# Hybrid decoder step on one Trainium2 core: order of work in the two inner layer norms, the state update on VectorE, and the wait for the last gated chunk

## The chip, the cores and the metric

One core of a Trainium2 chip runs the whole program. The time is device microseconds of that core for one launch. The core has TensorE (matmuls, called PE in the profile), VectorE (DVE), ScalarE (ACT), GpSimd (POOL) and SyncE (SP), which only issues transfers. Each engine is a queue that works in order; they are tied together by semaphores alone. Of the kernel before there are three timed runs and one profiled execution.

## The reference

One inference step of a hybrid decoder layer on 256 prompt tokens and 8 sample tokens, 264 columns in all, model width 2048, everything in float32:

```
h  = layer_norm(ALPHA * x  + mixer(x),            ln 0)   # gated DeltaNet heads + block-sparse attention
h  = layer_norm(ALPHA * h  + cross_attend(h),     ln 1)   # 4 heads, 256 memory tokens
y  = layer_norm(ALPHA * h  + swiglu(h),           ln 2)   # (silu(h W1a) * (h W1b)) W2, hidden 5632
layer_norm(x) = (x - mean(x)) * rsqrt(var(x) + 1e-5) * g + b
# recurrent state of every sample token b and head:
S  = S * exp(g_b) + k_b (outer) u_b
```

The mean and the variance are taken over the 2048 features of each token. The new states S of the eight samples (8 heads of 128 x 128 each) are an output too.

## The kernel before

**Layout.** Activations lie with features on the 128 partitions: `xf` is 16 chunks of 128 features by 264 tokens. Every float32 product is made from three faster ones: weights and activations are split into a rounded upper part (`wh`, `xh`) and the rest (`wl`, `xl`), and TensorE adds `wh*xh + wh*xl + wl*xh` (lines 504 to 506).

**Units.** A unit is one 128-column output tile: 16 chunks of weights, 1 MB, and 48 matmuls into one half of `psum_g`. For each unit SP loads `raw` (`load_unit`, line 477), ScalarE makes the upper part `wh` (`upper`, line 481), VectorE the low part `wl` (`lower`, line 486), and TensorE multiplies (`unit`, line 512). There are two slots of each. `upper` of unit U waits until unit U-2 has left TensorE; a load waits until the low part of two units before is made. `upper_next` and `lower_next` prepare the unit after the one named. The order of all that is written out by hand in each engine's program; nothing reorders it. The stages, with their units, are: `out` (16, mixer output), `wk` (4, memory keys), `xq` (4, queries), `wv` (4, memory values), `xo` (4, attention output), then `w1a` 32, `w2a` 16, `w1b` 32, `w2b` 16, `w1c` 24, `w2c` 16.

**Layer norm i** is spread over three engines. TensorE sums over the features by matmuls with a matrix of ones: sum in bank 0 of `M`, sum of squares in bank 1 (`gathered`, `last_sum`, `last_square`, lines 2118 to 2137). VectorE (line 1635) makes mean, mean square, variance and maximum with 0; ScalarE (line 1085) turns it into `rstd` by Ln and Exp. The 16 chunks are worked in five groups (`LN_PARTS`: 2, 2, 4, 4, 4 chunks): VectorE centres and scales a group, ScalarE applies g and b (line 1096) and rounds it to `xh` (line 1103), VectorE makes `xl` (line 1664). Layer norm 0 stands beside the four `wk` units, which need only the memory tokens; so the upper and low parts of the next units and the copies of finished keys (`memory_keys`, line 1118) are placed between the groups. The first `xq` unit waits group by group for the low parts. Layer norm 1 has no such unit beside it: the first `w1a` unit follows it. Between them ScalarE loads its table for Silu (line 1092).

**Before layer norm 1**, the four `xo` units each make four output chunks (banks 0 to 3 of `M`, or 4, 5 and both halves of `psum_g`). VectorE adds each to the residual `xf` and gathers sums in `xt[:, 8:12]` and squares in `xt[:, 12:16]`.

**Gate stages** (`w1a`, `w1b`, `w1c`): units come in pairs, gate and up. ScalarE makes Silu of the first, VectorE the product and its upper and low part, `gh` and `gl` (`gate_unit`, lines 1788 to 1800). **Residual stages** (`w2a`, `w2b`, `w2c`) multiply the 16 (or 12) gated chunks; their loops begin behind one wait for all low parts (line 2260).

**State update.** In `w1a`, 32 units in four turns of eight, the states of the eight samples are updated, one per four units: Pool loads state and rows into `state` and `ub`; VectorE scales the state (line 1811), ScalarE scales the rows by k, one instruction for each of 8 heads (line 1186), VectorE adds (line 1816), Pool stores. They hang on the semaphores `h_act` and `h_dve`.

Of the kernel before, what the change touches and what calls it, by code (L numbers as in the profile page):

```python
# [30 lines left out]
ACT = mybir.ActivationFunctionType  # L31
ALU = mybir.AluOpType
AXX = mybir.AxisListType.X
ds = bass.ds
# [7 lines left out]
H = 8  # L42
# [91 lines left out]
def build(nc, a, o):  # L134

    ctx = ExitStack()
    with ctx:
# [274 lines left out]
        h_act, h_dve = steps("h_act", ["k"]), steps("h_dve", ["g", "s"])  # L412
# [11 lines left out]
        NG = len(LN_PARTS)  # L424
        l_pe = steps("l_pe", ["sum", "var"])
# [6 lines left out]
        x_pe = steps("x_pe", ["sc", "ss", "pt", "st", "v0", "out", "v1", "so"])  # L432
        x_act = steps("x_act", ["exp", "sexp", "pt", "mv", "oh", "row0", "row1", "soh"])
        x_dve = steps("x_dve", ["qz", "mx", "smx", "rc", "src", "spn", "pn", "xpz", "mv", "ol", "row2", "row3", "sol"])
# [146 lines left out]
        def _(sp):  # L581
# [232 lines left out]
        def _(act):  # L814
# [270 lines left out]
            def layer_norm(i, between={}):  # L1085
# [5 lines left out]
                if i == 1:  # L1091
                    act.preload_act_table(ACT.Silu)
                for g, part in enumerate(LN_PARTS):
# [10 lines left out]
                    if g in between:  # L1104
                        between[g]()
# [12 lines left out]
            def memory_keys(u):  # L1118
# [47 lines left out]
            for u in range(4):  # L1166
                upper_next(act, turn, u)
                act.wait_ge(psum_free, 4 * turn + u + 3)
                if u >= 2:
                    act.wait_ge(sq_added, SUMS[1] + u - 1)  # L1170
                nc.scalar.activation(xt[:, 4 * (u % 2):4 * (u % 2) + 4], xf[:, 4 * u:4 * u + 4],
                                     ACT.Square).then_inc(sq_made, 1)
            layer_norm(1)
            turn, n = STAGES["w1a"]
            with act.Fori(0, n // 2) as i:
                for s in range(2):
                    for u in range(4):
                        upper_next(act, i * 2 + (turn + s), u)
                        if u % 2 == 0:
                            unit_done(act, i * 2 + (turn + s), u)  # L1180
                            act.wait_ge(psum_free, i * 8 + (4 * (turn + s) + u + 2))
# [7 lines left out]
            for s1_, s2_, first, nk in GROUPS:  # L1189
                if s1_ != "w1a":  # L1190
                    turn, n = STAGES[s1_]
                    with act.Fori(0, n) as i:
                        for u in range(4):
                            upper_next(act, i + turn, u)
                            if u % 2 == 0:
                                unit_done(act, i + turn, u)
                                act.wait_ge(psum_free, i * 4 + (4 * turn + u + 2))
                                nc.scalar.activation(sg[:], psum_g[:, 0, 0:T], ACT.Silu).then_inc(psum_free, 1)  # L1198
# [1145 lines left out]
```

## Time and profile before

| | |
|---|---|
| timed runs | 1705.89, 1713.7, 1715.07 us; median 1713.7 |
| profiled execution | 1706.84 us, of which the span from first to last instruction is 1705.2 |
| TensorE busy | 1583.8 us (93%), 14865 matmuls, mean granted clock 0.978 |
| VectorE, ScalarE busy | 886.2 us (52%), 648.8 us (38%) |
| low parts, line 489 | 223 instructions, mean 2287 ns |
| upper parts, line 484 | 223 instructions, mean 1874 ns |
| first matmul of a chunk, line 504 | idle 58.0 us before it, 24.2 of them for the low part of the weights |

How to read it: the busy time of TensorE counts overlapping records, so it is not the array's use; what counts is where it stands idle, and what ended that idle time. The last column of a timeline row, in brackets, is the idle time of the engine before the instruction and the instruction that ended it. The clock is given as a share of full speed.

### The profile page before, as it was taken

The page shows a single profiled execution, that of the slowest core. Times are in us where ns is not written, and L with a number is a line of the kernel's source. Part 1 is how long each engine was busy: PE and PEld are TensorE (multiplying, and loading weights), DVE is VectorE, ACT ScalarE, POOL GpSimd, SP SyncE. Part 2 cuts the span into 40 slices and gives each one's busy share as a digit, 9 for nine tenths or more (in the row PEclk, how much of TensorE's full clock was granted, in tenths as well). Part 3 has the DMA queues.
Part 4 walks back from the last instruction along what each step waited for, and adds up shares of the span by engine and source line. Part 5 has one row for each costly group of instructions (what it writes and reads, how often), then busy time and mean ns, then how long its engine had stood idle before and what let it go on. Part 6 is the DMA issues. An engine that isn't in the chain of part 4 may idle for free.

```text
span 1705.2 us, 36365 instructions
## 1 busy us (share of the span) xinstructions
PE 1583.8 (93%) x14865; PEld 1534.6 (90%) x14865; DVE 886.2 (52%) x992; ACT 648.8 (38%) x756; POOL 200.9 (12%) x298
## 2 busy tenths in 40 slices
PE   5989999999899879988978999999999999999996
PEld 5988999999889779987778999999999999999996
DVE  2435555656744246654476555444454444454466
ACT  3433334243422534443355344333333333333344
POOL 0001112121587501000100110000000000000000
PEclk9999999999999999988999999999999999999998
DMA  5589878685688967433644756545545544554443
GB/s 213 180 327 361 333 271 311 249 312 190 186 245 256 297 248 296 173 123 127 247 145 164 259 209 237 190 173 176 190 175 175 194 172 174 179 189 175 169 155 121
DMA packets 104415, 365.10 MB, mean 214 GB/s; under 512 B 14369, under 2 KB 48490, under 8 KB 77290
## 3 DMA queue, kind: packets, MB, share of 16 engines
q1 hardware_dynamic: 88978, 322.26, 53.2%
q0 software_dynamic: 12528, 37.24, 6.4%
q10 hardware_dynamic: 2800, 4.09, 0.8%
q8 instruction: 75, 1.23, 0.3%
q14 instruction: 34, 0.28, 0.0%
HBM read 353.27 MB, written 10.47 MB: 213 GB/s over the span
## 4 chain that ended last, share of the span: by engine, by line
PE 69%; issue 8%; DVE 7%; ACT 6%; SPq 3%; DMA 3%; POOL 2%; POOLq 1%; ACTq 1%; DVEq 0%
PE psum_g L504 20%; PE psum_g L505 19%; PE psum_g L506 19%; PE M L1910 4%; PE M L1895 3%; DVE wl L489 3%; ACT wh L484 3%; SPq L599 2%; PE psum_g L2193 1%; DMA raw<-w_out_t 1%; POOL pj L576 1%; ACT xf L1096 1%; ACT ub L1186 1%; DMA kring<-cache_k_t 1%; SPq L632 1%
## 5 line engine op out<-in xcount | busy, mean ns | idle before, releaser
L504 PE MATMUL psum_g<-xh,wh 128*128 128x264 f32 x2640 | 777.7, 295 | 58.0 <-DVE wl L489 24.2
L505 PE MATMUL psum_g<-xl,wh 128*128 128x264 f32 x2640 | 755.1, 286 | 0.0
L506 PE MATMUL psum_g<-xh,wl 128*128 128x264 f32 x2640 | 754.0, 286 | 0.0
L489 DVE TENSOR_TENSOR wl<-raw,wh 128x2048 fp32r<-128x2048 f32 (+1 forms) x223 | 510.1, 2287 | 445.7 <-ACT wh L484 445.4
L504 PEld LDWEIGHTS psum_g<-xh,wh 128*128 128x128 f32 x2640 | 503.9, 191 | 75.8 <-DVE wl L489 26.8
L484 ACT CAST wh<-raw 128x2048 fp32r<-128x2048 f32 (+1 forms) x223 | 417.8, 1874 | 318.0 <-PE psum_g L506 267.9
L505 PEld LDWEIGHTS psum_g<-xl,wh 128*128 128x128 f32 x2640 | 504.6, 191 | 3.4 <-issue 3.2
L506 PEld LDWEIGHTS psum_g<-xh,wl 128*128 128x128 f32 x2640 | 501.9, 190 | 0.0
L504 PE MATMUL psum_g<-gh,wh 128*128 128x264 f32 x704 | 202.0, 287 | 6.0 <-DVE gl L1798 6.0
L506 PE MATMUL psum_g<-gh,wl 128*128 128x264 f32 x704 | 200.9, 285 | 0.0
L505 PE MATMUL psum_g<-gl,wh 128*128 128x264 f32 x704 | 200.8, 285 | 0.0
L504 PEld LDWEIGHTS psum_g<-gh,wh 128*128 128x128 f32 x704 | 134.0, 190 | 6.8 <-issue 6.6
L505 PEld LDWEIGHTS psum_g<-gl,wh 128*128 128x128 f32 x704 | 134.1, 190 | 0.0
L506 PEld LDWEIGHTS psum_g<-gh,wl 128*128 128x128 f32 x704 | 133.4, 190 | 0.0
L1910 PE MATMUL M<-chain 128*128 128x128 f32 x704 | 90.2, 276 | 0.0
L1910 PEld LDWEIGHTS M<-chain 128*128 128x128 f32 x704 | 85.2, 193 | 0.0
L1895 PE MATMUL M<-kring,pj 128*32 128x128 f32 x1536 | 63.8, 277 | 9.9 <-DMA sraw<-cache_k_t 5.2
L1895 PEld LDWEIGHTS M<-kring,pj 128*32 128x32 f32 x1536 | 55.4, 111 | 15.6 <-issue 12.5
L744 POOL TENSOR_TENSOR chain<-chain,C 128x512 f32<-128x512 f32 x28 | 43.0, 1537 | 122.4 <-PE M L1910 101.1
L576 POOL DMA_DIRECT2D pj<-cache_v x102 | 54.7, 538 | 10.8 <-issue 6.1
L1836 DVE SCALAR_TENSOR_TENSOR xf<-xf,psum_g 128x264 f32 (+1 forms) x48 | 20.6, 429 | 64.8 <-PE psum_g L506 64.5
L1198 ACT ACTIVATE sg<-psum_g 128x264 f32<-128x264 f32 x28 | 11.0, 391 | 111.1 <-PE psum_g L506 111.1
(380 smaller groups left out, 1312.0 us busy)
## 6 DMA issues: line engine op xcount, KB each, us to landing
raw<-w_t SPq DMA_DIRECT2D x88, 1024.0 KB, 4.8
raw<-w_in_t SPq DMA_DIRECT2D x55, 1024.0 KB, 6.7
kring<-cache_k_t SPq DMA_DIRECT2D x96, 512.0 KB, 4.5
sraw<-cache_k_t SPq DMA_DIRECT2D x32, 512.0 KB, 6.0
raw<-w_out_t SPq DMA_DIRECT2D x16, 1024.0 KB, 4.8
raw<-w2a_t SPq DMA_DIRECT2D x16, 1024.0 KB, 4.8
raw<-w2b_t SPq DMA_DIRECT2D x16, 1024.0 KB, 4.7
raw<-w2c_t SPq DMA_DIRECT2D x16, 768.0 KB, 4.2
```

The costliest lines, as they stand in the source:

```text
L484: nc.scalar.copy(wh[:, u % 2, 0:nk], raw[:, u % 2, 0:nk]).then_inc(hi_done, 1)
L489: eng.tensor_tensor(wl[:, u % 2, 0:nk], raw[:, u % 2, 0:nk], wh[:, u % 2, 0:nk].bitcast(F32), ALU.subtract).then_inc(raw_used, 1)
L504: nc.tensor.matmul(out, hi_w, x_hi(k), start=(k == order[0]), stop=False)
L505: nc.tensor.matmul(out, hi_w, x_lo(k), start=False, stop=False)
L506: last = nc.tensor.matmul(out, lo_w, x_hi(k), start=False, stop=(k == order[-1]))
L576: eng.dma_start(v_pages[s][:, t], a["cache_v"][0, ds(pages[6 * n_ + t], 1), :, h].rearrange("a t d -> t (a d)"))\
L599: _, pages = nc.values_load_multi_w_load_instructions(page_turns[4 * i + u:4 * i + u + 1], engines={mybir.EngineType.SP}, min_val=0, max_v ...
L632: sp.dma_start(state_half(b, s), a["state_dn"][0, b, 4 * s:4 * s + 4].rearrange("h d e -> d h e"))\
L744: nc.gpsimd.tensor_tensor(cm, at0, over(mask), ALU.mult).then_inc(b_pool.sem, 1)
L1836: nc.vector.scalar_tensor_tensor(m, m, ALPHA if s2_ == "w2a" else 1.0, psum_g[:, u % 2, 0:T], ALU.mult, ALU.add).then_inc(psum_free, 1)
L1895: last = nc.tensor.matmul(M[rows:rows + 32, pg // 4, (pg % 4) * P:(pg % 4 + 1) * P], qz[:, b + 4 * (p % 2), h], k_slot(m)[:, h * P:(h + 1) ...
L1910: last = nc.tensor.matmul(out(w), lhs(w), rhs(w), start=True, stop=True)
```

## The change

Five edits.

1. **Layer norm 0.** ScalarE makes the upper part of the second `wk` unit before the layer norm's first step, and the others in hooks before group 0 and after groups 1 and 2. VectorE makes the low part of that unit behind the mean square, ahead of the variance, and the others after both first groups are scaled, and at the second and third group; its low passes and centre/scale passes are interleaved in another order.
2. **Layer norm 1 and the last `xo` unit.** VectorE takes the last unit's result in halves (`x_pe` "half"), adds the last four residual chunks to the running sum itself, and makes the next weights' low part only then. TensorE gathers the squares first, then one group of sums in place of two. ScalarE squares in halves. The order of VectorE's passes changes, and the Silu table load moves behind the whole layer norm.
3. **State update.** The eight ScalarE instructions per sample become one VectorE multiplication, behind the gate of the first pair. ScalarE's loop of `w1a` becomes the same as that of the other gate stages, eight turns of four units.
4. **Residual stages.** TensorE's first turn is written out; before chunk 0 it waits for all gated chunks but the last, and for the last one before the last chunk.
5. **Layer norm 2** works in groups of 4, 4, 4, 2, 2 chunks.

```diff
-        h_act, h_dve = steps("h_act", ["k"]), steps("h_dve", ["g", "s"])
+        h_dve = steps("h_dve", ["g", "k", "s"])
+        Y_PARTS = [slice(0, 4), slice(4, 8), slice(8, 12), slice(12, 14), slice(14, 16)]
+        def ln_parts(i):
+            return Y_PARTS if i == 2 else LN_PARTS
...
# ScalarE
-                if i == 1:
-                    act.preload_act_table(ACT.Silu)
-                for g, part in enumerate(LN_PARTS):
+                for g, part in enumerate(ln_parts(i)):
+                    if g in before:
+                        before[g]()
...
-                    if g in between:
-                        between[g]()
+                    if g in after:
+                        after[g]()
...
-            layer_norm(0, {0: lambda: upper_next(act, turn, 0), 1: lambda: memory_keys(0), 2: lambda: upper_next(act, turn, 1),
-                           3: lambda: (memory_keys(1), upper_next(act, turn, 2))})
-            memory_keys(2)
-            upper_next(act, turn, 3)
+            upper_next(act, turn, 0)
+            layer_norm(0, before={0: lambda: (memory_keys(0), upper_next(act, turn, 1))},
+                       after={1: lambda: (memory_keys(1), upper_next(act, turn, 2)),
+                              2: lambda: (memory_keys(2), upper_next(act, turn, 3))})
             memory_keys(3)
...
             layer_norm(1)
+            act.preload_act_table(ACT.Silu)
...
-                        if u == 0:
-                            act.wait_ge(h_ub[s], i * 16 + 16)
-                            for h in range(H):
-                                ins = nc.scalar.activation(ub[:, s, h], ub[:, s, h], ACT.Identity,
-                                                           scale=keep[:, 0, ds(i * 2 + s, 1), h:h + 1].rearrange("p a b -> p (a b)"))
-                            ins.then_inc(h_act.sem, 1)
...
# VectorE, layer norm
                 nc.vector.tensor_tensor(acc[:], mean[:], mean[:], ALU.mult).then_inc(l_dve.sem, 1)
+                at("msq")
...
                 scale(0)
                 scale(1)
-                at("vmax")
-                centre(2)
-                scale(2)
-                at("n2")
-                low(0)
-                low(1)
-                centre(3)
-                scale(3)
-                at("n3")
-                low(2)
-                centre(4)
-                scale(4)
+                at("n1")
+                if i == 0:
+                    low(0)
+                    centre(2)
+                    scale(2)
+                    low(1)
+                    at("n2")
+                    centre(3)
+                    scale(3)
+                    low(2)
+                    at("n3")
+                    centre(4)
+                    scale(4)
+                else:
+                    centre(2)
+                    low(0)
+                    scale(2)
+                    low(1)
+                    for g in (3, 4):
+                        centre(g)
+                        scale(g)
+                    low(2)
                 low(3)
                 low(4)
...
-            layer_norm(0, {"vmax": lambda: lower_next(dve, turn, 0), "n2": lambda: lower_next(dve, turn, 1),
-                           "n3": lambda: lower_next(dve, turn, 2)})
-            lower_next(dve, turn, 3)
+            layer_norm(0, {"msq": lambda: lower_next(dve, turn, 0), "n1": lambda: lower_next(dve, turn, 1),
+                           "n2": lambda: lower_next(dve, turn, 2), "n3": lambda: lower_next(dve, turn, 3)})
...
# VectorE, last xo unit
+            wait(dve, x_pe, "half")
+            nc.vector.scalar_tensor_tensor(xf[:, 12:14], xf[:, 12:14], ALPHA, M[:, 4:6, 0:T], ALU.mult, ALU.add).then_inc(x_dve.sem, 1)
+            unit_done(dve, turn, 3)
+            nc.vector.scalar_tensor_tensor(xf[:, 14:16], xf[:, 14:16], ALPHA, psum_g[:, :, 0:T], ALU.mult,
+                                           ALU.add).then_inc(psum_free, 1)
...
+            nc.vector.tensor_tensor(xt[:, 8:12], xt[:, 8:12], xf[:, 12:16], ALU.add).then_inc(x_dve.sem, 1)
+            lower_next(dve, turn, 3)
             layer_norm(1)
...
# VectorE, state update in w1a
+                        elif u == 1:
+                            dve.wait_ge(h_ub[s], i * 16 + 16)
+                            nc.vector.tensor_tensor(ub[:, s], ub[:, s], per_head(0, i * 2 + s), ALU.mult).then_inc(h_dve.sem, 1)
+                        elif u == 2:
+                            dve.wait_ge(h_dve.sem, i * 6 + (3 * s + 2))
                             nc.vector.tensor_tensor(state[:, s], state[:, s], ub[:, s], ALU.add).then_inc(h_dve.sem, 1)
...
# TensorE
-            gathered(1, at(xt, 8), at(xt, 12))
-            last_sum(1, turn, 4, at(xf, 12))
+            pe.wait_ge(sq_added, SUMS[2])
+            for j, x in enumerate(at(xt, 12)):
+                nc.tensor.matmul(M[:, 1, 0:T], ones, x, start=(j == 0), stop=False)
+            wait(pe, x_dve, "sum")
+            for j, x in enumerate(at(xt, 8)):
+                last = nc.tensor.matmul(M[:, 0, 0:T], ones, x, start=(j == 0), stop=(j == 3))
+            last.then_inc(l_pe.sem, 1)
             last_square(1, at(xt, 4))
...
-                pe.wait_ge(gl_done, first + nk + 2)
                 turn, n = STAGES[s2_]
-                with pe.Fori(0, n) as i:
+
+                def gated_up_to(k):
+                    if k in (0, nk - 1):
+                        pe.wait_ge(gl_done, first + nk + 1 + (k == nk - 1))
+
+                for u in range(4):
+                    unit(pe, turn, u, GH, GL, nk=nk, before=gated_up_to if u == 0 else lambda k: None)
+                with pe.Fori(1, n) as i:
                     for u in range(4):
-                        unit(pe, i + turn, u, lambda k: gh[:, k], lambda k: gl[:, k], nk=nk)
+                        unit(pe, i + turn, u, GH, GL, nk=nk)
```

## Rows read from the trace of the kernel before

**Rows 1.** Busy time by stretch: us, each engine busy (instructions), clock, DMA, GB/s.
```profile
1110.00:1378.00 268.00, 268.00 (x2221) 268.00 (x2219) 129.73 (x107) 92.33 (x62) 0.00 (x0) 1.00 0.51 180
```

**Rows 2.** Waits of TensorE over the whole span: us in total, times, longest.
```profile
PE psum_g L504 <- DVE gl L1798: 6.0, 3, 2.0
```

**Rows 3.** Timeline of TensorE, layer norm 0: start, us, instruction, [idle before].
```profile
750.68 0.58 PE L504 MATMUL psum_g<-mem_h,wh 128*128 128x256 f32 x1 [5.86 <-DVE wl L489]
...
760.52 0.39 PE L504 MATMUL psum_g<-mem_h,wh 128*128 128x256 f32 x1 [1.94 <-DVE wl L489]
...
783.14 0.59 PE L504 MATMUL psum_g<-xh,wh 128*128 128x264 f32 x1 [3.80 <-DVE wl L489]
```

**Rows 4.** Timeline of ScalarE, layer norm 0.
```profile
742.88 0.42 ACT L1088 ACTIVATE rstd<-rstd 128x264 f32<-128x264 f32 x1 [4.62 <-DVE rstd L1646]
...
753.12 2.10 ACT L1096 ACTIVATE xf<-xf,ln_gb 128x264 f32<-128x264 f32 x4 [2.88 <-DVE xf L1656]
755.26 1.08 ACT L1103 CAST xh<-xf 128x1056 fp32r<-128x1056 f32 x1
...
792.02 0.39 ACT L1133 ACTIVATE xq<-psum_g 128x264 f32<-128x264 f32 x1 [9.18 <-PE psum_g L506]
```

**Rows 5.** Timeline of VectorE, layer norm 0.
```profile
740.61 0.43 DVE L1640 TENSOR_TENSOR acc<-mean 128x264 f32<-128x264 f32 x1
...
748.34 2.29 DVE L489 TENSOR_TENSOR wl<-raw,wh 128x2048 fp32r<-128x2048 f32 x1 [3.02 <-ACT wh L484]
750.54 1.25 DVE L1650 TENSOR_TENSOR xf<-xf,mean 128x1056 f32<-128x1056 f32 x1
```

**Rows 6.** Transfers, layer norm 0: count, KB each, median us to landing.
```profile
raw<-x_wk_t SPq DMA_DIRECT2D x4, 1024.0 KB, 4.8
```

**Rows 7.** TensorE in 2 us steps, layer norm 0: busy (matmuls), clock, DMA.
```profile
763.00:765.00 2.00, 2.00 (x11) 0.50 0.82 344
```

**Rows 8.** The chain that ended last, before layer norm 1: start, us, instruction.
```profile
876.92 1.78 PE M L2122 x8
```

**Rows 9.** Timeline of VectorE, layer norm 1.
```profile
884.15 0.43 DVE L1643 SCALAR_TENSOR_TENSOR rstd<-M,acc 128x264 f32<-128x264 f32 x1 [0.95 <-PE M L2136]
```

**Rows 10.** Timeline of ScalarE, layer norm 1.
```profile
885.84 1.28 ACT L1092 ACT_TABLE_LOAD   x1
887.14 1.10 ACT L1096 ACTIVATE xf<-xf,ln_gb 128x264 f32<-128x264 f32 x2
...
900.59 1.89 ACT L484 CAST wh<-raw 128x2048 fp32r<-128x2048 f32 x1
```

**Rows 11.** Timeline of TensorE, layer norm 1.
```profile
890.62 0.56 PE L504 MATMUL psum_g<-xh,wh 128*128 128x264 f32 x1 [6.58 <-DVE xl L1664]
...
905.32 0.39 PE L504 MATMUL psum_g<-xh,wh 128*128 128x264 f32 x1 [1.56 <-DVE wl L489]
```

**Rows 12.** Timeline of TensorE, first gate stage.
```profile
960.68 0.39 PE L504 MATMUL psum_g<-xh,wh 128*128 128x264 f32 x1 [1.31 <-DVE wl L489]
```

**Rows 13.** Timeline of ScalarE, first gate stage.
```profile
953.98 2.44 ACT L1186 ACTIVATE ub<-ub,C 128x128 f32<-128x128 f32 x8
```

**Rows 14.** Timeline of VectorE, first gate stage.
```profile
948.98 0.43 DVE L1798 TENSOR_TENSOR gl<-gu,gh 128x264 f32 x1
...
952.16 1.22 DVE L1811 TENSOR_TENSOR state<-state,C 128x1024 f32<-128x1024 f32 x1
```

**Rows 15.** All waits in the first gate stage, those of the Pool queue.
```profile
POOL out_dn_sample L807 <- DVE state L1816: 195.2, 8, 64.4
```

**Rows 16.** Timeline of TensorE, first residual stage.
```profile
1098.45 0.38 PE L504 MATMUL psum_g<-gh,wh 128*128 128x264 f32 x1 [1.98 <-DVE gl L1798]
```

**Rows 17.** TensorE in 2 us steps, first residual stage.
```profile
1100.00:1102.00 2.00, 2.00 (x11) 0.50 0.10 16
1102.00:1104.00 2.00, 2.00 (x14) 0.67 0.73 274
```

**Rows 18.** Timeline of ScalarE, last layer norm.
```profile
1700.01 2.10 ACT L1096 ACTIVATE xf<-xf,ln_gb 128x264 f32<-128x264 f32 x4 [0.36 <-DVE xf L1656]
```

More of the change, by code:

```diff
@@ L431, in build @@
         x_pool = steps("x_pool", ["zero"])
-        x_pe = steps("x_pe", ["sc", "ss", "pt", "st", "v0", "out", "v1", "so"])
+        x_pe = steps("x_pe", ["sc", "ss", "pt", "st", "v0", "out", "v1", "so", "half"])
         x_act = steps("x_act", ["exp", "sexp", "pt", "mv", "oh", "row0", "row1", "soh"])
-        x_dve = steps("x_dve", ["qz", "mx", "smx", "rc", "src", "spn", "pn", "xpz", "mv", "ol", "row2", "row3", "sol"])
+        x_dve = steps("x_dve", ["qz", "mx", "smx", "rc", "src", "spn", "pn", "xpz", "mv", "ol", "row2", "row3", "sol", "half", "sum"])
         gh_done, gl_done = sem("gh_done"), sem("gl_done")
@@ L697, in _ @@
                         load_unit(sp, i + turn, u, w_tile(a[s2_ + "_t"], i * 4 + u), nk)
-            for g, part in enumerate(LN_PARTS):
+            for g, part in enumerate(Y_PARTS):
                 sp.wait_ge(y_ready, g + 1)
@@ L1083, in square, with layer_norm @@
                 nc.scalar.activation(xt[:, u % 2], m, ACT.Square).then_inc(sq_made, 1)
-            def layer_norm(i, between={}):
+            def layer_norm(i, before={}, after={}):
                 wait(act, l_dve, "vmax", i)
@@ L1167, in _ @@
                 upper_next(act, turn, u)
-                act.wait_ge(psum_free, 4 * turn + u + 3)
                 if u >= 2:
                     act.wait_ge(sq_added, SUMS[1] + u - 1)
+                if u == 3:
+                    wait(act, x_dve, "half")
+                    nc.scalar.activation(xt[:, 4:6], xf[:, 12:14], ACT.Square)
+                    act.wait_ge(psum_free, 4 * turn + u + 3)
+                    nc.scalar.activation(xt[:, 6:8], xf[:, 14:16], ACT.Square).then_inc(sq_made, 1)
+                    continue
+                act.wait_ge(psum_free, 4 * turn + u + 3)
                 nc.scalar.activation(xt[:, 4 * (u % 2):4 * (u % 2) + 4], xf[:, 4 * u:4 * u + 4],
@@ L1173, in _ @@
             layer_norm(1)
[L1174 to L1176 removed]
+            act.preload_act_table(ACT.Silu)
+            for s1_, s2_, first, nk in GROUPS:
+                turn, n = STAGES[s1_]
+                with act.Fori(0, n) as i:
                     for u in range(4):
[L1178 removed]
+                        upper_next(act, i + turn, u)
                         if u % 2 == 0:
[L1180 to L1181 removed]
+                            unit_done(act, i + turn, u)
+                            act.wait_ge(psum_free, i * 4 + (4 * turn + u + 2))
                             nc.scalar.activation(sg[:], psum_g[:, 0, 0:T], ACT.Silu).then_inc(psum_free, 1)
[L1183 to L1198 removed]
                 turn, n = STAGES[s2_]
@@ L1767, in _ @@
             turn, n = STAGES["xo"]
-            for u in range(4):
+            for u in range(3):
                 lower_next(dve, turn, u)
@@ L1785, in _ @@
                                             ALU.add).then_inc(sq_added, 1)
+            wait(dve, x_pe, "half")
[3 more added lines that the diff above has]
+                                           ALU.add).then_inc(psum_free, 1)
+            wait(dve, x_dve, "half")
+            dve.wait_ge(psum_free, 4 * turn + 6)
+            dve.wait_ge(sum_done, SUMS[2])
+            nc.vector.tensor_tensor(xt[:, 8:12], xt[:, 8:12], xf[:, 12:16], ALU.add).then_inc(x_dve.sem, 1)
+            lower_next(dve, turn, 3)
             layer_norm(1)
@@ L1800, in gate_unit, with per_head @@
                                         ALU.subtract).then_inc(gl_done, 1)
+            def per_head(which, b):
+                return keep[:, which, ds(b, 1)].rearrange("p a h -> p (a h)").unsqueeze(2).to_broadcast([P, H, P])
             turn, n = STAGES["w1a"]
```

16 lines of the change are left out of this document (7 added, 9 removed).

## The prediction

> **What bounds the kernel now.** I read four views in this order: the page's shares, the busy time by stretch, the waits of TensorE, then the timeline of each engine around those waits. The page puts TensorE at 93% and the other engines at 52% or less. The windows show what that means where nothing disturbs it: from 1110 to 1378 us TensorE is busy 268.0 of 268.0 us, 2221 matmuls, 0.12 us each, so a unit (16 chunks x 3 products = 48 matmuls) takes 5.8 us [rows 1]. The order of the other engines matters only where TensorE stands still. The reader should look for such places inside the parts that the diff touches. There are four: the memory-key projection beside layer norm 0 (gaps of 5.86 and 1.94 us, a third of 3.9 not shown, and 3.80 [rows 3]); layer norm 1 (6.58 us, then 1.56 before the second unit after it [rows 11]); one gap of 1.31 us per sample in the first gate stage, seven of them, of which one row stands [rows 12]; and three waits of 2.0 us for the last gated chunk [rows 2].
>
> Gaps also cost afterwards. Where there are none the granted clock is 1.00 [rows 1]; behind the 1.94 us gap it is 0.50 [rows 7]. That is the lower of TensorE's two levels, 1.2 against 2.4 GHz. The unit that begins at 750.68 ends at 758.58 (760.52 less its gap): 7.9 us instead of 5.8. The unit from 783.14 ends about 791.9, when ScalarE copies its result [rows 3, 4]: 8.8 us.
>
> **Layer norm 0.** Before, ScalarE finishes the last square at 738.26 and then waits for the statistics [rows 4]. It rounds the weights of memory unit 1 only after the first normalised group, so VectorE makes their low part at 748.34, and TensorE starts at 750.68 instead of 744.8, when unit 0 ended [rows 3, 5]. Three more units are held up in the same way. I rebuilt the new order with unchanged durations: upper part 1.9 us [rows 10], low part 2.2 to 2.3 [rows 5], passes over four chunks 1.25 [rows 5], the affine step plus cast of four chunks 3.2 [rows 4].
> - Unit 1: upper part 738.2 to 740.1; low part after the mean square, 741.0 to 743.3 [rows 5]. TensorE goes on at 744.8 with no gap. This pushes variance, maximum and centring back by 1.3 us (VectorE is one queue), and the scaling starts at 745.2.
> - Unit 2: ScalarE copies key 0 at 744.9 and makes the upper part to 747.2; low part 747.2 to 749.5; needed at 750.6.
> - Unit 3: upper part 751.1 to 753.0; low part 753.2 to 755.5 behind the first low pass, the third group's centre and scale and the second low pass; needed at 756.4.
> - First query unit: upper part to 758.8, low part 759.2 to 761.4; TensorE reaches it at 762.2. Its first eight chunks have their low parts by 759.1. Chunks 8 to 11 are ready at 765.1. The last four need centre 4, scale 4 (763.9), ScalarE's group (767.1) and the low pass (768.4): TensorE waits 1.9 us and ends the unit at 770.0.
> - Second query unit: ScalarE is free at 767.5, upper part to 769.4, low part to 771.7; a gap of 1.75 us, start 771.75.
> The same start was 791.9 before, so the gain is 20.1 us. Each earlier low part also frees a weight slot earlier, and SP issues the next load then (for units 2 and 3 and for the queries). A 1 MB load lands in 4.8 us [rows 6]. Memory unit 3, loaded from 743.3, would be there at 748.1 for an upper part at 751.1, which is 3 us of cover. The two gaps that stay lie close together, 3.65 us idle out of 5.2, and a gap of 1.94 was enough for half clock [rows 3, 7]. The cost is between nothing and 3.0 us, what the unit behind 3.80 us lost. I take 1.7, on the side of the short gap. Layer norm 0: +18.4.
>
> **Layer norm 1 and the unit before it.** TensorE's statistics are four groups of four matmuls, 1.78 us each (one group is x8 in the chain of waits) [rows 8]. Before, two groups are gathered, then the last sum, then the last square, and the variance is read at 884.15 [rows 9]. Now the sum's last part is added on VectorE (1.25), which removes one group (1.8) from TensorE but must wait for the residual update after the unit. The squares' group runs meanwhile to 878.7; the added sum is ready at 879.05; the sum's group ends at 880.9, the last square at 882.7. The low part of the next weights now lies behind the sum (879.05 to 881.3), so it delays the mean but not the variance, at 882.8: 1.35 us earlier. The Silu table load (1.28) leaves the place before the first affine step, where it held it until 887.14 [rows 10]. VectorE's new order gives: first low part 887.8 instead of 890.6, third 895.7 (it now comes behind the centring and scaling of all groups), fourth 896.9, last 899.9. So TensorE starts 2.8 us earlier, waits about 5 us at chunk 4, and can end the unit between 901.9 and 903.2, depending on how long the clock stays low. That end decides nothing, for the second unit's upper part is behind the last cast and the table load: 898.6 + 1.25 = 899.85 instead of 900.59 [rows 10]. TensorE can start at 904.6 instead of 905.32 [rows 11]: +0.7. The wait before it grows, and half clock there would cost up to 2.1, what the unit after 5.86 us lost. I take -0.7, and 0 in sum, bounds -2 and +1.
> The table load lasts 1.28 us and the next ScalarE instruction starts 0.02 behind its end, at 887.14 [rows 10]. The Trainium skill, "ScalarE: Activation LUTs", What ACT_TABLE_LOAD costs, puts a drain of about 1.38 us on top of each switch. By that rule the second unit would start at 906.0, later than before, and this part would be -1.4; the trace shows no such drain, so the sum doesn't use it.
>
> **State update in the first gate stage.** Before, eight ScalarE instructions per sample scale the rows, 2.44 us together, right before the upper part of the next unit [rows 13]. Upper part plus low part need 1.9 + 2.3 of a unit's 5.8 us, so only 1.6 us are spare, and with 0.39 for the Silu the 2.44 us overrun them: the gap is 1.31 [rows 12]. Now it is one VectorE instruction of the same form and size as the state's scaling: 1.22 us [rows 14]. It stands behind the gate's three operations. They end at 949.41, 1.7 us after their unit ended (two units before 959.37) [rows 12, 14]. The new one then runs to 2.9, the next low part to 5.2, and TensorE wants it at 5.8: 0.6 us of cover. If that is gone the gap returns, smaller. The instruction also waits for its row transfer; behind it are the low part and all of TensorE. But the Pool queue waited 195.2 us for VectorE's result in this stage, up to 64.4 at a time [rows 15], so the data of both slots lie there long before. Gain 7 x 1.31 = 9.2, bounds 0 (the overrun just moves to VectorE) and 9.2.
>
> **Residual units.** Only the last chunk's low part is late, and chunk 15 is 45 matmuls, 5.4 us, after chunk 0; the gate needs 1.7. So all three waits of 2.0 go [rows 2, 16], 6.0 us. After the first wait the clock is 0.50 for 2 us, then 0.67 on the mean of 2 more: 2 x 0.50 + 2 x 0.33 = 1.7 us of work lost, taken as 1.6 [rows 17]. The third wait has the same shadow, the second has none. Together 9.2, bounds 6.0 and 9.2. What is late next is the low part of the second residual unit, behind the gate at 1.7 + 2.3 = 4.0 of 5.8 us: hidden. To do this the first turn of three TensorE loops is written out (576 matmuls), while the ScalarE loop of the first gate stage takes eight turns instead of four.
>
> **Last layer norm.** Its parts are 4, 4, 4, 2, 2 chunks instead of 2, 2, 4, 4, 4. VectorE ends at the same time, and ScalarE's last piece shrinks from 2.10 [rows 18] to 1.1; but its first group starts 1.7 us later, and 16 chunks at 0.53 from 1693.75 end at 1702.2, as before. Only the last store is smaller: +0.2, bounds -0.5 and +1.
>
> **Sum.** 18.4 + 0 + 9.2 + 9.2 + 0.2 = 37.0 us. The profiled execution took 1706.84 us (span 1705.2 and 1.64 around it), so it would be 1669.8. The three timed runs lie at 1705.9, 1713.7 and 1715.1. With the median of 1713.7 it is 1676.7. I can't tell which of these levels a new median meets and predict the middle, 1673. The likely case's own range is 1665 to 1680.
>
> **Rivals.**
> 1. *Half clock stays where the gaps were.* The two gaps of 1.9 and 1.75 us in layer norm 0, the longer ones in layer norm 1, cost in full: 3.0 instead of 1.7 there, -2 instead of 0 here, and the 3.2 us of half clock behind the waits for the last chunk stay as well. For it: gaps of 1.94 did this. Against: in the gate stage gaps of 1.31 never did. Gain 37.0 - 6.5 = 30.5, time 1679.5.
> 2. *VectorE becomes the bound in the gate stage.* The 0.6 us of cover is gone by waits between its instructions, so the 9.2 us shrink to 0 or little. For it: three gate operations, a multiplication and a low part in one row. Against: at 52% of the span it has air, and all of its durations are steady. Gain 28, time 1682.
> 3. *Layer norm 0 gives back half.* A low part late by over 1 us at memory unit 3 or at the first query (their cover is 0.9 and 0.8 us) puts the later ones back too, since each engine is one queue. Gain 27, time 1683.
> 4. *Slower.* The written-out units and the extra loop turns stall instruction supply. Place: the jumps back in the loops of the feed-forward part, some 35 for TensorE. It decides if each jump costs over 37 / 35 = 1.06 us: at 1.6 us each it takes 35 x 1.6 = 56, and the time is 1673 + 56 = 1729. Against: loops of the same four-unit body run now without a microsecond of idle time in 268 us [rows 1].
> The Trainium skill, "Runtime: NRT & Kernel Launch", Instruction fetch mechanics, states such a rule: a taken branch outside the fetched window forces a fetch. By that rule the present loops, with the same jumps, should already stall; rows 1 show none.
>
> **Chances.** Forecast 0.66; rival 1 0.11; rival 2 0.09; rival 3 0.11; rival 4 0.02; 0.01 for a change that does nothing measurable. A difference under 0.5%, 8.6 us, can't be told from none. Forecast and rivals 1 to 3 are all faster by more: 0.96 with a little taken off for mixes; within 0.5% 0.02, slower 0.02. The range takes in rivals 1 to 3 and, below, the 1670 level with the clock kept high: 1663 to 1687.
>
> **What would show it.** Right: the memory units follow each other with no gap in TensorE and the second query unit starts near 772; in the first gate stage TensorE has no gap at a low part; no wait for the last gated chunk, and the granted clock is 1.00 behind all three; behind layer norm 1 the first unit starts nearly 3 us less late, the second only 0.7. Wrong: gaps ahead of memory unit 2 or 3 (rival 3); low parts that start behind the row multiplication and end after TensorE is free (rival 2); clock 0.50 in the query units (rival 1); idle time of TensorE put down to issue at loop jumps (rival 4). Should the layer norm 0 stretch gain under 15 us, my rebuilt order is wrong.

## The result and the profile after

| | before | after |
|---|---|---|
| median of 4 runs | 1711.86 us | 1667.66 us |
| lowest, highest | 1705.89, 1715.07 | 1664.38, 1672.9 |
| profiled execution, span | 1706.84, 1705.2 | 1664.38, 1662.7 |
| mean granted clock | 0.978 | 0.985 |

The ratio is 0.9749, 95% interval 0.9709 to 0.9788: faster. The medians differ by 44.2 us and the profiled executions by 42.5 us of span, where 37.0 were worked out. Timed again, five runs against nine, the medians differ by 41.0 us (1670.25 against 1711.27). The range held the time; the likely case's own range, 1665 to 1680, did too.

The mixer, ahead of every edit, takes more or less time by itself from one execution to the next: the last residual update before layer norm 0 starts at 736.5 us in this execution and between 739.1 and 748.5 in those of the experiments. So each part below is measured between two instructions that enclose it, not by the end of the span. These are the points, of the kernel before:

```profile
737.37 0.43 DVE L1699 SCALAR_TENSOR_TENSOR xf<-xf,psum_g 128x264 f32<-128x264 f32 x1 [0.45 <-PE psum_g L506]
...
851.69 0.39 PE L504 MATMUL M<-xh,wh 128*128 128x264 f32 x1 [0.50 <-DVE xl L1763]
...
870.84 0.39 PE L504 MATMUL M<-xh,wh 128*128 128x264 f32 x1 [0.41 <-DVE wl L489]
```

They are the last residual update before layer norm 0, the first matmul of the attention output, and the first of its last unit. The same three after:

```profile
736.54 0.43 DVE L1706 SCALAR_TENSOR_TENSOR xf<-xf,psum_g 128x264 f32<-128x264 f32 x1 [0.45 <-PE psum_g L511]
...
830.41 0.39 PE L509 MATMUL M<-xh,wh 128*128 128x264 f32 x1 [0.50 <-DVE xl L1769]
...
851.08 0.39 PE L509 MATMUL M<-xh,wh 128*128 128x264 f32 x1 [0.40 <-DVE wl L494]
```

**Layer norm 0, after.** The timeline of TensorE shows only two gaps left where there were four [rows 3], ahead of the last four chunks of the first query unit and of the second query unit. No gap stands before any memory unit.

```profile
767.33 0.39 PE L509 MATMUL psum_g<-xh,wh 128*128 128x264 f32 x1 [1.66 <-DVE xl L1661]
...
770.43 0.39 PE L509 MATMUL psum_g<-xh,wh 128*128 128x264 f32 x1 [1.38 <-DVE wl L494]
```

The timeline of VectorE is the one that the prediction rebuilt. The first four low parts of weights follow their upper parts at once or stand in an unbroken row of passes; only the last low pass (766.01) waits, 2.11 us for ScalarE's cast, and behind it the weights of the second query unit:

```profile
740.12 2.28 DVE L494 TENSOR_TENSOR wl<-raw,wh 128x2048 fp32r<-128x2048 f32 x1
...
746.24 2.29 DVE L494 TENSOR_TENSOR wl<-raw,wh 128x2048 fp32r<-128x2048 f32 x1 [0.69 <-ACT wh L489]
...
752.15 2.28 DVE L494 TENSOR_TENSOR wl<-raw,wh 128x2048 fp32r<-128x2048 f32 x1
...
757.98 2.29 DVE L494 TENSOR_TENSOR wl<-raw,wh 128x2048 fp32r<-128x2048 f32 x1
...
766.01 1.26 DVE L1661 TENSOR_TENSOR xl<-xf,xh 128x1056 fp32r<-128x1056 f32 x1 [2.11 <-ACT xh L1108]
768.08 2.29 DVE L494 TENSOR_TENSOR wl<-raw,wh 128x2048 fp32r<-128x2048 f32 x1 [0.81 <-ACT wh L489]
```

From the last residual update to the second query unit it takes 770.43 - 736.54 = 33.9 us; before it was 791.9 - 737.37 = 54.5 [rows 4]. The gain is 20.6. The busy time of TensorE in 2 us steps (us, busy and matmuls, clock, DMA share, GB/s) shows that neither gap brought the clock down:

```profile
766.00:768.00 2.00, 0.67 (x5) 1.00 0.00 0
...
770.00:772.00 2.00, 1.57 (x13) 1.00 0.42 66
772.00:774.00 2.00, 2.00 (x19) 1.00 0.87 360
```

But it fell at the start of the attention output, where two short gaps stand in both kernels (1.23 and 0.50 us) and the one before kept 1.00:

```profile
832.00:834.00 2.00, 2.00 (x11) 0.50 0.95 289
834.00:836.00 2.00, 2.00 (x16) 0.88 0.91 297
```

The first three of the four output units take 851.08 - 830.41 = 20.7 us instead of 870.84 - 851.69 = 19.15.

**Layer norm 1, after.** TensorE, VectorE, ScalarE, in this order:

```profile
859.30 2.05 PE L2276 MATMUL M<-xt,C 128*128 128x264 f32 x8 [0.37 <-DVE xt L1800]
...
868.55 0.56 PE L509 MATMUL psum_g<-xh,wh 128*128 128x264 f32 x1 [5.42 <-DVE xl L1661]
...
876.34 0.59 PE L509 MATMUL psum_g<-xh,wh 128*128 128x264 f32 x1 [4.41 <-DVE xl L1661]
...
884.73 0.39 PE L509 MATMUL psum_g<-xh,wh 128*128 128x264 f32 x1 [1.10 <-DVE wl L494]
...
863.24 0.43 DVE L1640 SCALAR_TENSOR_TENSOR rstd<-M,acc 128x264 f32<-128x264 f32 x1 [0.95 <-PE M L2156]
...
879.05 1.28 ACT L1185 ACT_TABLE_LOAD   x1
880.35 1.90 ACT L489 CAST wh<-raw 128x2048 fp32r<-128x2048 f32 x1
```

The first gate unit begins 17.5 us after the last output unit (868.55 - 851.08), before 19.8 [rows 11], then stops 4.41 us at chunk 4. The second, the one that counts, begins after 33.65 us instead of 34.5.

**First gate stage, after.** One sample on VectorE: gate, scaling of the rows (L1833), next low part, with no idle time in brackets behind the gate.

```profile
915.21 0.43 DVE L1814 TENSOR_TENSOR gl<-gu,gh 128x264 f32 x1
915.56 1.22 DVE L1833 TENSOR_TENSOR ub<-ub,C 128x1024 f32<-128x1024 f32 x1
916.70 2.29 DVE L494 TENSOR_TENSOR wl<-raw,wh 128x2048 fp32r<-128x2048 f32 x1
```

The low part ends at 918.9 (it holds VectorE for 2.2 us), and TensorE wants it when the running unit ends, which is at 919.8: ScalarE's Silu of that unit starts at 919.92. TensorE has no gap left in the stage. The Pool queue still waits for VectorE, as in [rows 15]:

```profile
POOL out_dn_sample L812 <- DVE state L1836: 185.6, 8, 65.7
```

**Residual stages and the end.** From 1050 to 1640 us, across all three groups, TensorE is busy all the time at full clock; the waits of [rows 2, 16] are gone, and so is the shadow of [rows 17], as the stretch of half clock behind a gap is called here. In the last layer norm ScalarE starts later than before and then never stops.

```profile
1050.00:1640.00 590.00, 590.00 (x4880) 1.00 0.52 179
...
1652.11 8.08 ACT L1101 ACTIVATE xf<-xf,ln_gb 128x264 f32<-128x264 f32 x16 [2.63 <-DVE xf L1653]
```

The first matmul of the last layer norm's statistics, after, is one more point for the table:

```profile
1645.34 0.61 PE L2142 MATMUL M<-acc,C 128*128 128x264 f32 x2
```

**Where the 42.5 us are.** By these points, before against after, in us:

| stretch | before | after | gain | predicted |
|---|---|---|---|---|
| to the last update before layer norm 0 | 737.4 | 736.5 | 0.8 | 0 |
| to the second query unit | 54.5 | 33.9 | 20.6 | 18.4 |
| to the attention output | 59.8 | 60.0 | -0.2 | 0 |
| its first three units | 19.15 | 20.7 | -1.5 | 0 |
| last output unit to the second gate unit | 34.5 | 33.65 | 0.8 | 0 |
| to the first residual unit | 193.1 | 179.9 | 13.2 | 9.2 + 2.0 |
| to the statistics of layer norm 2 | 588.4 | 580.7 | 7.7 | 7.2 |
| to the end | 18.3 | 17.4 | 1.0 | 0.2 |

The first row lies ahead of every edit, so 0.8 of the 42.5 us is no gain of the change.

### The profile page after: what moved, and what is told of

Read it like the earlier page. It is cut to its first block, busy times and chain, and to the rows that moved or that the text cites. A ratio compares the mean times of both kernels' runs of the same rounds, so it can differ in the third digit from the quotient of the medians.

```text
span 1662.7 us, 36222 instructions
## 1 busy us (share of the span) xinstructions
PE 1568.5 (94%) x14857; PEld 1521.8 (92%) x14857; DVE 897.3 (54%) x1001; ACT 629.9 (38%) x693; POOL 201.5 (12%) x298
## 4 chain that ended last, share of the span: by engine, by line
PE 74%; issue 7%; DVE 5%; ACT 5%; SPq 3%; DMA 3%; POOL 2%; POOLq 1%; ACTq 1%; DVEq 0%
PE psum_g L509 21%; PE psum_g L510 21%; PE psum_g L511 21%; PE M L1930 4%; PE M L1915 3%; DVE wl L494 2%; ACT wh L489 2%; SPq L637 1%; SPq L604 1%; ACT xf L1101 1%; PE psum_g L2213 1%; DMA raw<-w_out_t 1%; DMA kring<-cache_k_t 1%; DMA raw<-w_in_t 1%; POOL pj L581 1%
## 5 line engine op out<-in xcount | busy, mean ns | idle before, releaser
L1194 ACT ACTIVATE sg<-psum_g 128x264 f32<-128x264 f32 x44 | 17.2, 391 | 172.2 <-PE psum_g L511 172.2
L916 ACT COPY pj<-psum_g 128x264 f32<-128x264 f32 x24 | 9.1, 378 | 113.4 <-PE psum_g L511 113.4
```

## The experiments

Each is the changed kernel with one edit taken back or done in another way. Where a ratio is given it is to the kernel before, timed on the same chip; the changed kernel timed so once more gave 0.9767 (0.974 to 0.9793), median 1670.25 us against 1711.27.

**1. Old order in layer norm 0.** VectorE's low passes go back to their old places between centring and scaling as well; the lines below do not show that.

```diff
-            upper_next(act, turn, 0)
-            layer_norm(0, before={0: lambda: (memory_keys(0), upper_next(act, turn, 1))}, ...
+            layer_norm(0, after={0: lambda: upper_next(act, turn, 0), 1: lambda: memory_keys(0), ...
-            layer_norm(0, {"msq": lambda: lower_next(dve, turn, 0), "n1": lambda: lower_next(dve, turn, 1), ...
+            layer_norm(0, {"n1": lambda: lower_next(dve, turn, 0), "n2": lambda: lower_next(dve, turn, 1), ...
```

> The changed kernel with the old order of work in layer norm 0 alone (upper and low parts of the memory units, and the interleaving of the low passes). Theory (the whole gain of this stretch is the order): from the last residual update before the layer norm to the start of the second query unit it takes about 54.5 us again instead of 33.9, and the kernel is 20 to 21 us slower than the changed one, about 24 us faster than the kernel before. Rival (part of the gain came from elsewhere, as an earlier load): the stretch stays below 50 us.

Measured: 1691.04 us, ratio 0.9883 (0.9844 to 0.9921). The four gaps of TensorE are back:

```profile
758.07 0.58 PE L509 MATMUL psum_g<-mem_h,wh 128*128 128x256 f32 x1 [5.86 <-DVE wl L494]
...
767.91 0.58 PE L509 MATMUL psum_g<-mem_h,wh 128*128 128x256 f32 x1 [2.56 <-DVE wl L494]
...
779.25 0.58 PE L509 MATMUL psum_g<-mem_h,wh 128*128 128x256 f32 x1 [3.92 <-DVE wl L494]
...
790.53 0.39 PE L509 MATMUL psum_g<-xh,wh 128*128 128x264 f32 x1 [2.80 <-DVE wl L494]
```

The stretch from the last update (744.76) to the second query unit, which starts as the first one's result is copied at 798.2, is 53.4 us: 19.5 more than in the changed kernel, and to the attention output 857.89 - 744.76 = 113.1 against 93.9, so 19.3. The theory holds; the expected 20 to 21 was 1 us high because the first query unit, at half clock for a part in both, takes 7.7 us here and took 8.8 in the kernel before; the second of its gaps was longer, 2.56 us instead of 1.94. So the order is worth 19.4 to 20.6 us, by how long the clock stays low in the gaps' shadow.

**2 and 3. The rows scaled on ScalarE, in two places.**

```diff
+                        if u == 0:        # experiment 2; in experiment 3: if u == 1:
+                            act.wait_ge(h_ub[s], i * 16 + 16)
+                            for h in range(H):
+                                ins = nc.scalar.activation(ub[:, s, h], ub[:, s, h], ACT.Identity, ...)
+                            ins.then_inc(h_act.sem, 1)
```

> The changed kernel with the scaling of the rows back on ScalarE, eight instructions in the old place behind the Silu of the first unit of four, and ScalarE's loop back at four turns of eight units. Theory (a gap costs more than its idle time, since the restart of the pipeline is not counted in it): seven gaps of 1.31 us idle, but each period of four units takes 24.8 instead of 23.2 us, so the stage is about 11 us longer, not 9.2. Rival (the rest came from elsewhere): 9.2 us.

> The same, with the eight ScalarE instructions behind the upper part made in the second unit of four, where no Silu stands and ScalarE idles 3.5 us. Theory (it is the place in ScalarE's queue that cost, not the engine): no gap, each four units take 23.2 us, and the stage and the kernel are as fast as with VectorE. Rival (ScalarE has no room for 2.44 us per four units): gaps of about 1.3 us come back, 11 us in all.

Measured: in the even unit 1684.7 us, ratio 0.9845 (0.9819 to 0.9872). In the odd unit 1674.42, ratio 0.9797 (0.977 to 0.9825), and timed once more:

> ScalarE's eight instructions in the odd unit once more, now timed on the same chip as the changed kernel. Theory (place, not engine): within 0.3% of the changed kernel. Rival: 0.6% slower.

Measured: 1671.82 us, ratio 0.977 (0.9749 to 0.9791), next to 0.9767 for the changed kernel on the same chip. The first fence is TensorE with the even place, the second ScalarE with the odd one.

```profile
925.77 0.39 PE L509 MATMUL psum_g<-xh,wh 128*128 128x264 f32 x1 [1.32 <-DVE wl L494]
...
950.56 0.39 PE L509 MATMUL psum_g<-xh,wh 128*128 128x264 f32 x1 [1.31 <-DVE wl L494]
```

```profile
908.54 1.91 ACT L489 CAST wh<-raw 128x2048 fp32r<-128x2048 f32 x1 [3.53 <-PE psum_g L511]
914.43 0.39 ACT L1194 ACTIVATE sg<-psum_g 128x264 f32<-128x264 f32 x1 [3.97 <-PE psum_g L511]
914.71 1.90 ACT L489 CAST wh<-raw 128x2048 fp32r<-128x2048 f32 x1
916.51 2.45 ACT L1198 ACTIVATE ub<-ub,C 128x128 f32<-128x128 f32 x8
```

With the even place the gaps are 1.31 us again, but they come every 24.79 us, where four units without a gap take 23.2, so each costs 1.6. From the second gate unit to the first residual unit it is 1086.2 - 895.07 = 191.1 us; with VectorE and with ScalarE's odd place it is 179.9 both (1064.64 - 884.73, 1070.7 - 890.83). In the odd unit the same 2.45 us lie behind the upper part, where ScalarE otherwise idles 3.5 us (as the 3.53 and 3.97 us before the rows at 908.54 and 914.43 show). The theory holds against its rival: what cost 11 us was the place in ScalarE's queue, and moving it to VectorE was one of two cures.

**4. One wait for all gated chunks, first turn still written out.**

```diff
-                    if k in (0, nk - 1):
-                        pe.wait_ge(gl_done, first + nk + 1 + (k == nk - 1))
+                    if k == 0:
+                        pe.wait_ge(gl_done, first + nk + 2)
```

> The changed kernel with all gated chunks, the last one too, waited for before chunk 0 in each residual stage; the first turn of the loops stays written out. Theory (the wait and its shadow of half clock are the whole gain): three gaps of 2.0 us, each 0.27 more with the restart, and half clock behind some of them at 1.6 us each: 6.8 to 11.6 us slower than the changed kernel. Rival (the written-out turn brought it): no more than 3 us slower.

Measured: 1681.2 us, ratio 0.9836 (0.9809 to 0.9864). Waits of TensorE and the clock in 3 us steps behind the first and the second:

```profile
1069.18 0.36 PE L509 MATMUL psum_g<-gh,wh 128*128 128x264 f32 x1 [1.79 <-DVE gl L1814]
...
1351.17 0.36 PE L509 MATMUL psum_g<-gh,wh 128*128 128x264 f32 x1 [1.81 <-DVE gl L1814]
...
1070.00:1073.00 3.00, 3.00 (x16) 0.53 0.32 117
...
1352.00:1355.00 3.00, 3.00 (x28) 1.00 0.27 101
```

The three waits come back with 1.8 us idle each. From the second gate unit to the first residual unit it is 1.9 us longer (1069.18 - 887.33 = 181.85), from there to the first statistics matmul of the last layer norm 5.7 (586.4 against 580.7), 7.6 in sum. Three waits at 1.8 + 0.27 are 6.2; the rest, 1.4, goes with the half clock behind the first (0.53, where the second and the third kept 1.00). The written-out turn brought nothing of it.

**5 to 7. The parts of layer norm 1.** One execution each, profiled, read between the last output unit and the second gate unit (33.65 us in the changed kernel, 34.5 before).

```diff
# 5: statistics as before; the residual update in halves and the squares in halves go back too (not shown)
-            nc.vector.tensor_tensor(xt[:, 8:12], xt[:, 8:12], xf[:, 12:16], ALU.add).then_inc(x_dve.sem, 1)
+            gathered(1, at(xt, 8), at(xt, 12))
+            last_sum(1, turn, 4, at(xf, 12))
# 6: VectorE's old order of passes
-                    centre(2); low(0); scale(2); low(1); centre(3); scale(3); centre(4); scale(4); low(2)
+                    centre(2); scale(2); low(0); low(1); centre(3); scale(3); low(2); centre(4); scale(4)
# 7: table load before the first affine step
-            act.preload_act_table(ACT.Silu)       # behind layer_norm(1)
+                if i == 1:
+                    act.preload_act_table(ACT.Silu)
```

> The changed kernel with the statistics before layer norm 1 as in the kernel before (whole-tile residual update, four groups of statistics matmuls, next low part ahead of the update); the order within the layer norm and the table load stay changed. Theory (taking one group of 1.8 us off TensorE is partly eaten by the wait for VectorE's sum): from the start of the last output unit to the variance on VectorE 13.3 us as in the kernel before instead of 12.2, and the second gate unit starts about 1.1 us later. Rival (the statistics are hidden by something else): no difference at the second gate unit.

> The changed kernel with VectorE's old order of passes in layer norm 1 only. Theory (the second gate unit hangs on ScalarE's chain, which is fed as well by either order): the pause of 4.4 us before chunk 4 of the first gate unit shrinks to about 1.5, but the second gate unit starts within 0.5 us of the same place. Rival (the new order feeds ScalarE sooner): it starts over 1 us later.

> The changed kernel with the Silu table load back before the first affine step of layer norm 1. Theory (behind the layer norm the load is on the path to the upper part of the second gate unit, before it only holds back affine steps by a few tenths): the upper part starts about 1.0 us earlier and the second gate unit as well. Rival (the first affine step is held back and with it the whole chain): 0.3 or more later.

Measured, in the order of the fences: VectorE's variance and the second gate unit of 5; the first gate unit's chunk 4, the second gate unit and the clock behind it of 6; table load and upper part of 7.

```profile
866.78 0.43 DVE L1634 SCALAR_TENSOR_TENSOR rstd<-M,acc 128x264 f32<-128x264 f32 x1 [0.95 <-PE M L2140]
...
888.63 0.39 PE L509 MATMUL psum_g<-xh,wh 128*128 128x264 f32 x1 [2.23 <-DVE wl L494]
```

```profile
885.82 0.59 PE L509 MATMUL psum_g<-xh,wh 128*128 128x264 f32 x1 [1.18 <-DVE xl L1661]
...
897.17 0.55 PE L509 MATMUL psum_g<-xh,wh 128*128 128x264 f32 x1 [2.18 <-DVE wl L494]
...
898.00:900.00 2.00, 2.00 (x11) 0.50 0.72 221
```

```profile
870.13 1.28 ACT L1097 ACT_TABLE_LOAD   x1
...
884.48 1.90 ACT L489 CAST wh<-raw 128x2048 fp32r<-128x2048 f32 x1
```

- 5: the last output unit starts at 853.47, the variance comes 13.3 us later (after: 863.24 - 851.08 = 12.16) and the second gate unit 35.2 later. The rebuilt statistics as a whole, the added sum with the halves and the later low part, are worth 1.5 us at that unit, more than expected; the parts were not taken apart.
- 6: 863.05 to 897.17 is 34.1 us, 0.5 more than in the changed kernel. The pause at chunk 4 falls to 1.18 us, as the theory said, and is of no use. Behind the wait of 2.18 us the clock also fell to 0.50, and the first residual unit came 2.0 us later than in the changed kernel (215.6 us after the last output unit, against 213.6). The 1.5 us on top are not shown to belong to the order: waits of 2.23 us in experiment 5 and 2.33 in the repeat of 3, in the same place, were followed by clock 1.00.
- 7: the upper part starts 884.48 - 856.28 = 28.2 us after the last output unit, in the changed kernel 29.3, so 1.1 us sooner; TensorE then has no gap over 0.3 us there. The move of the table load was a loss.

At the second gate unit the three add up: 1.5 + 0.5 - 1.1 = 0.9, against the 0.8 between before and after.

**8. Old groups in the last layer norm.**

```diff
-            return Y_PARTS if i == 2 else LN_PARTS
+            return LN_PARTS
```

> The changed kernel with the old groups in the last layer norm. Theory (the smaller last store lands sooner and ScalarE ends 0.4 us sooner): from the first statistics matmul of the last layer norm to the end of the span 18.3 us instead of 17.4. Rival (noise): no difference.

Measured: from the first statistics matmul (1650.18) to the end (1668.5) 18.3 us, after 17.4, the theory. ScalarE ends at 1665.4, 15.2 us after that matmul, in the changed kernel 14.8 (1660.2 less 1645.34), so 0.4 us are ScalarE and 0.6 the smaller last store.

**9. The changed kernel again, and a version that prepares the next unit inside the layer norm.**

```diff
+                              3: lambda: (memory_keys(3), upper_next(act, STAGES["xq"][0], 0))})
...
+            upper_next(act, STAGES["w1a"][0], 0)      # ScalarE, before layer_norm(1)
...
                 low(3)
+                at("lo3")                              # VectorE: the low part of that unit
                 low(4)
```

> The changed kernel once more, as the base for the next two. Both theories: as before, ratio 0.975 to the kernel before; the first two attention output units take 14.2 us, at half clock for a part, as in the other runs with the new order in layer norm 0.

> The changed kernel with the weights of the unit behind each layer norm prepared inside it: the second query unit's upper part behind group 3 and its low part ahead of the last low pass, the second gate unit's upper part in ScalarE's idle time before layer norm 1 and its low part ahead of the last low pass; the first turn of the first gate stage written out on ScalarE and VectorE. Theory (both gaps are queues in the wrong order and nothing else): no gap before either unit, at a price of 0.5 to 0.75 us in the last low pass; 0.9 + 0.8 = 1.7 us faster than the changed kernel, ratio to it 0.999, below what 5 rounds can tell, so it is read from the stretches. Rival (the low pass of the last group is the bound): no gain.

Measured: 1670.25 us and 1665.46, ratios 0.9767 (0.974 to 0.9793) and 0.9734 (0.9706 to 0.9761); the intervals overlap. The first two output units took 848.05 - 833.86 = 14.2 us in the changed kernel, as expected. Of the eleven profiled executions with the new order in layer norm 0 seven show 14.2, and four show 12.7 as both executions with the old order do, the kernel before and experiment 1: experiments 5 and 7, the repeat of 3, and this version (854.40 - 841.75). So the half clock there comes and goes with the same code; that the new order makes it likelier is neither shown nor excluded. VectorE, TensorE and its clock in the new version, layer norm 0:

```profile
774.82 2.28 DVE L494 TENSOR_TENSOR wl<-raw,wh 128x2048 fp32r<-128x2048 f32 x1
777.44 1.26 DVE L1671 TENSOR_TENSOR xl<-xf,xh 128x1056 fp32r<-128x1056 f32 x1 [0.34 <-ACT xh L1108]
...
778.76 0.39 PE L509 MATMUL psum_g<-xh,wh 128*128 128x264 f32 x1 [2.07 <-DVE xl L1671]
...
780.00:782.00 2.00, 2.00 (x11) 0.50 0.58 246
```

There is no gap before the second query unit, but the last low pass starts 0.4 us later (29.9 against 29.5 us after the last update), so the first query unit waits 2.07 us and ends 781.26 - 747.54 = 33.7 us after the last update, where the second one started at 33.9 before. The attention output begins after 94.2 us instead of 93.9, so there is no gain, as the rival said, but not for the rival's reason. Behind the wait of 2.07 us the clock fell to 0.50. From that wait to the end of the first query unit it took 2.5 us, where the changed kernel took 1.7 at full clock, and the second query unit took 6.6 us instead of 5.8: 1.6 us in all. By these rows the order alone would be about 1.3 us ahead (an estimate: 94.2 - 1.6 = 92.6 against 93.9). No run shows how often the clock falls at this wait. Behind layer norm 1 the gap before the second gate unit closes as the theory has it, while the waits of the first gate unit (5.42 and 4.41 us) stay: 1073.1 - 860.88 = 212.2 us from the last output unit to the first residual unit instead of 213.6. The net is about 1 us, which the timed ratio can't tell.

## Why the prediction was right, and where its sizes were off

- **Layer norm 0** (18.4, measured 20.6). The rebuilt order was right to 0.3 us in the low parts of all memory units and 0.5 in those of the queries (counted from the last update); gaps forecast at 1.9 and 1.75 were 1.66 and 1.38. Off was the term for the clock: 1.7 us taken for half clock behind them, none came (clock 1.00). The bound "nothing" was the true one: in all ten executions with these two gaps the clock behind them was 1.00. Experiment 1 shows the order, with the clock's shadow, as 19.4.
- **Layer norm 1** (0, bounds -2 and 1; measured 0.8). The second gate unit was forecast 0.7 us earlier and came 0.8 earlier; the 0.7 us set against it for half clock did not come, since the clock behind its wait of 1.10 us was 1.00. The variance came 1.15 us earlier, forecast 1.35, and the rebuilt statistics were worth 1.5 at that unit (experiment 5). The table load on the path was forecast and is shown to cost 1.1 (experiment 7). No drain followed it: the next instruction starts at 880.35, 0.02 us behind the end of the load. The rule of the Trainium skill, "ScalarE: Activation LUTs", What ACT_TABLE_LOAD costs, does not agree with this trace either, and the measurement decides.
- **State update** (9.2, measured 11.2). The step "7 x 1.31" was mis-sized: the price of a gap is read from the period of the pattern, 24.79 - 23.2 = 1.6 us, not from the idle time in the row. The record of a matmul lasts 0.28 us where the next one follows after 0.12, so 0.16 is hidden before the idle time starts, and the restart adds 0.11 (first record 0.39 instead of 0.28). The cover of 0.6 us for the new VectorE instruction was 0.9. That ScalarE's place was the cause is shown (experiments 2, 3).
- **Residual units** (9.2, measured 2.0 + 7.7 = 9.7). The waits and two shadows of half clock went, each wait with the same 0.27 more, 0.8 in all, which covers the difference of 0.5. Experiment 4 has the waits back with one shadow: 7.6.
- **Last layer norm** (0.2, measured 1.0; its bound was 1). Both terms were mis-sized: ScalarE was to end as before, at 0.53 us for a chunk, but its unbroken row of 16 chunks took 8.08 us, 0.505 each, and ended 0.4 us sooner, and the smaller store was worth 0.6 (experiment 8).
- **The rivals.** Rival 1 did not happen where it was placed; half clock for part of two output units cost 1.5 us in the profiled execution, and by experiment 9 it comes and goes with the same code. Rivals 2 and 3: none of the low parts that they name was late. The low part that is late in the stretch of layer norm 0, ahead of the second query unit, was forecast so. Rival 4: 590 us of loops and written-out turns without idle time. The rule of the Trainium skill, "Runtime: NRT & Kernel Launch", Instruction fetch mechanics, has a stall at a taken branch whose target lies outside the fetched window; no run shows whether the targets here lie outside it, and none shows a stall in these loops.
- **The level.** The median came out 5 us below the predicted 1673, which was the middle of 1669.8 and 1676.7. The profiled execution came out 5.5 below its 1669.8, of which 0.8 lies ahead of every edit. The forecast parts gave 2.2 + 0.8 + 2.0 + 0.5 + 0.8 = 6.3 us more than worked out; 1.5 + 0.2 us in and ahead of the output units, which the sum had at nothing, went the other way, so errors cancelled in part.

## What to carry to other kernels

Where one engine should never stop and two others feed it, look at the place of each piece in the feeders' queues before changing who does it: the same 2.45 us on ScalarE cost 11 us in the unit with the Silu and nothing in the next. Rebuild the order by hand from measured durations, with cover in each step; it held to a few tenths here. Price a recurring gap by the period of its pattern, since the idle time in a row of TensorE leaves 0.27 us out.

## What the runs showed of the hardware

- Short gaps of like length bring TensorE's clock to 0.50 at one time and not at the next: of three waits of 1.8 us one was followed by half clock, of three of 2.0 two, and of waits of 2.18, 2.23 and 2.33 us in one place only that of 2.18. The two gaps of 1.66 and 1.38 us close together had clock 1.00 behind them in all ten executions that have them, while the pair of 1.23 and 0.50 us ahead of the attention output was followed by half clock in seven of all thirteen.
- One unit of 48 matmuls takes 5.8 us at full clock, and each gap of the first gate stage costs its idle time, 1.31 us, and 0.27 us more.
- The table load of ScalarE takes 1.28 us in both of its places, and the next instruction starts 0.02 us behind its end.
